# Latent attention: one key product for two heads, and swapped rotary columns among the query weights

## What is computed

```python
def apply_rope(x, cos, sin):
    x1, x2 = jnp.split(x, 2, axis=-1)
    return jnp.concatenate([x1 * c - x2 * s, x2 * c + x1 * s], axis=-1)

def mla_project(q_lat, kv_lat, g_qa, w_qb, g_kva, w_kvb):      # 384 and 256 latents
    q = (rms_norm_2(q_lat, g_qa) @ w_qb).reshape(B, T, 8, 64 + 32)
    kv = (rms_norm_2(kv_lat, g_kva) @ w_kvb).reshape(B, T, 8, 64 + 64)
    return q[..., :64], q[..., 64:], kv[..., :64], kv[..., 64:]
...
qr_x = apply_rope(qr_x, cos_b, sin_b)                          # 32 rotary columns of a head's query
kr_x = apply_rope(krb_x[:, :, None, :], cos_b, sin_b)[:, :, 0] # 32 rotary columns, one key for all heads
s = einsum(q_n, keys_n) + einsum(q_r, keys_r)                  # 64 + 32 = 96 columns
o = softmax(s * 96 ** -0.5) @ vals
```

## Time and profile before

| what | us |
| --- | --- |
| three runs | 3919.3, 3922.16, 3916.91 |
| their median | 3919.3 |
| the profiled execution, its own time | 3926.21 |
| its span, from the first to the last instruction | 3924.3 |

### The profile page before, as it was taken

How to read it: one execution, slowest core, us unless ns; L and a number is a source line. 1 busy time by engine, 2 the same in 40 slices (tenths; PEclk the granted TensorE clock), 3 DMA queues, 4 the chain that set the end, 5 groups by cost and what they waited for, 6 DMA issues and landing times.

```text
span 3924.3 us, 54000 instructions
## 1 busy us (share of the span) xinstructions
PE 3676.7 (94%) x21015; PEld 3094.3 (79%) x21015; DVE 2169.5 (55%) x4547; ACT 1419.9 (36%) x2285; POOL 761.6 (19%) x645
## 2 busy tenths in 40 slices
PE   6989998979999997999997999999999879999997
PEld 4877886869898997999985568868888645776885
DVE  3353343598998667777874463274343345436443
ACT  3223323324444442333333452263222335425322
POOL 0000000007987864555530000000000000000000
PEclk8999999999999999999998999999999989989998
DMA  5223323458787889999971001101111210210222
GB/s 214 92 76 140 102 97 119 156 188 288 272 306 265 300 306 364 347 343 344 372 286 54 33 28 59 60 1 54 65 65 60 102 33 33 73 62 22 97 98 85
DMA packets 220555, 594.49 MB, mean 151 GB/s; under 512 B 17936, under 2 KB 101520, under 8 KB 215952
## 3 DMA queue, kind: packets, MB, share of 16 engines
q1 hardware_dynamic: 156592, 380.68, 28.3%
q0 software_dynamic: 36864, 134.23, 9.5%
q10 hardware_dynamic: 26848, 76.14, 5.1%
HBM read 530.16 MB, written 60.82 MB: 151 GB/s over the span
## 4 chain that ended last, share of the span: by engine, by line
PE 79%; DVE 9%; DMA 7%; issue 2%; ACT 2%; POOL 1%; ACTq 0%; DVEq 0%; SPq 0%
PE bank L735 62%; PE bank L934 6%; DMA WR<-in_vrows 4%; PE bank L1028 3%; PE bank L1014 3%; PE bank L901 2%; DVE WL L1502 1%; PE bank L759 1%; PE bank L796 1%; DMA rows<-in_urows,rk 1%; POOL rows L666 1%; DMA WR<-in_weights 1%; DMA rows<-in_vrows,rk 1%; DVE Rw L1763 1%; ACT WH L1119 0%
## 5 line engine op out<-in xcount | busy, mean ns | idle before, releaser
L1502 DVE TENSOR_TENSOR WL<-WR,WH 128x1024 fp32r<-128x1024 f32 x512 | 631.1, 1234 | 821.2 <-ACT WH L1119 767.2
L1119 ACT ACTIVATE WH<-WR 128x1024 fp32r<-128x1024 f32 x512 | 537.0, 1057 | 798.7 <-DMA WR<-in_weights 201.4
L735 PE MATMUL bank<-H2h,WH 128*128 128x512 f32 (+2 forms) x1624 | 578.6, 356 | 4.5 <-DVE H2l L1530 4.5
L735 PE MATMUL bank<-H2h,WL 128*128 128x512 f32 (+2 forms) x1624 | 573.6, 353 | 0.0
L735 PE MATMUL bank<-H2l,WH 128*128 128x512 f32 (+2 forms) x1624 | 573.0, 353 | 0.0
L735 PE MATMUL bank<-Hh,WH 128*128 128x384 f32 (+1 forms) x1440 | 527.5, 366 | 23.6 <-DVE WL L1502 23.5
L735 PE MATMUL bank<-Hh,WL 128*128 128x384 f32 (+1 forms) x1440 | 512.4, 356 | 0.0
L735 PE MATMUL bank<-Hl,WH 128*128 128x384 f32 (+1 forms) x1440 | 511.7, 355 | 0.0
L934 PE MATMUL bank<-ah,WH 128*128 128x384 f32 x1024 | 345.1, 337 | 35.3 <-issue 18.6
L666 POOL DMA_INDIRECT rows<-in_urows,rk x128 | 169.5, 1324 | 968.4 <-DVE rk L1788 744.4
L735 PEld LDWEIGHTS bank<-H2h,WH 128*128 128x128 f32 (+1 forms) x1624 | 307.0, 189 | 52.5 <-issue 7.7
(11 more groups left out here) (310 smaller groups left out, 5778.8 us busy)
## 6 DMA issues: line engine op xcount, KB each, us to landing
WR<-in_weights SPq DMA_DIRECT2D x498, 512.0 KB, 3.8
WR<-in_vrows SPq DMA_DIRECT2D x128, 512.0 KB, 9.2
gelu_by_expert<-geU ACTq DMA_DIRECT2D x128, 192.0 KB, 5.0
gates_by_expert<-tab ACTq DMA_DIRECT2D x24, 1024.0 KB, 6.4
geV<-gelu_by_expert SPq DMA_DIRECT2D x32, 768.0 KB, 11.8
Gt<-gates_by_expert SPq DMA_DIRECT2D x16, 1536.0 KB, 18.5
x_kept<-X ACTq DMA_DIRECT2D x2, 3072.0 KB, 8.7
X<-x_kept ACTq DMA_DIRECT2D x2, 3072.0 KB, 11.3
```

The costliest lines, as they stand in the source:

```text
L735: yield nc.tensor.matmul(b[0:rows, out_cols], a, r, start=n == 0, stop=n == len(pairs) - 1)
L1119: act.activation(WH[:, n % SLOTS, :, :].rearrange("p a b -> p (a b)"), WR[:, c % SLOTS, :, :].rearrange("p a b -> p (a b)"), ACT.Copy)\
L1502: v.tensor_tensor(WL[:, n % SLOTS, :, :].rearrange("p a b -> p (a b)"), WR[:, plan.splits[n] % SLOTS, :, :].rearrange("p a b -> p (a b)"), ...
```

## The change

The query weights of a head get 32 more columns: the rotary columns again, with their halves swapped. The query product of x so has 128 rows, and rows 96 to 127 are what the permutation product gave, apart from a sign, which goes into the sin table. DVE reads both parts from the bank. The same is done for the shared rotary key. The jobs `hqp` and `krbp`, the matrix `permB`, its load, and the copies to `R4` are gone, and the banks of `hq` and `krb` for x belong to DVE now. The key product is made for two heads at a time, at even h, with 128 rows; ACT copies the upper half into the slot of head h + 1 and the lower half into that of head h. A second tile of two key slots, `KH2`, is added, so that four heads' keys have room. A chunk is still loaded for every head.

```diff
@@ CONSTS
-CONSTS = [("ident", 128), ("perm128", 128), ("permA", 128), ("permB", 96), ("iota128", 128), ("fold", 3)]
+CONSTS = [("ident", 128), ("perm128", 128), ("permA", 128), ("iota128", 128), ("fold", 3)]
@@ make_plan, project
             p.chunk(("hb", l, h), ("hb", l, h), False)
-            p.job(("hq", l, h, "x"), "A")
+            p.job(("hq", l, h, "x"), "V", [] if upd or h % 2 == 0 else [("hb", l, h)])
             if upd:
-                p.job(("hq", l, h, "c"), "A")
-            p.job(("hk", l, h, "x"), "A")
-            p.job(("hk", l, h, "c"), "A", [("hb", l, h)])
-            p.job(("hqp", l, h), "V")
+                p.job(("hq", l, h, "c"), "A", [] if h % 2 == 0 else [("hb", l, h)])
+            if h % 2 == 0:
+                p.job(("hk", l, h, "x"), "A")
+                p.job(("hk", l, h, "c"), "A", [("hb", l, h)])
@@ make_plan, queries_b
-            p.job(("krb", l, "x"), "A")
+            p.job(("krb", l, "x"), "V")
             p.job(("krb", l, "c"), "A", [("krb", l)])
-            p.job(("krbp", l), "V")
@@ build
+        KH2 = place("KH2", B0 + 19200, 2, A)
...
+        def keys_of(h):
+
+            return (KH, KH2)[h % 4 // 2][:, h % 2, :]
@@ PE, project
-                    wq = w[:, 0:QL * QKB].rearrange("p (k n) -> p k n", k=QL)
-                    wk = w[:, QL * QKB:QL * QKB + KVL * NOPE].rearrange("p (k n) -> p k n", k=KVL)
+                    wq = w[:, 0:QL * P].rearrange("p (k n) -> p k n", k=QL)
+                    wk = w[:, QL * P:(QL + KVL) * P].rearrange("p (k n) -> p k n", k=KVL)
                     for c in xc:
+                        rows_ = P if c == "x" else QKB
                         product(("hq", l, h, c), slice(0, T if c == "x" else C),
-                                [(wq[:, j, :], LAT[:, j, xcols(c)]) for j in range(QL)], QKB)
-                    for c in ("x", "c"):
+                                [(wq[:, j, 0:rows_], LAT[:, j, xcols(c)]) for j in range(QL)], rows_)
+                    for c in ("x", "c") if h % 2 == 0 else ():
                         product(("hk", l, h, c), slice(0, T if c == "x" else C),
-                                [(wk[:, j, :], LAT[:, QL + j, xcols(c)]) for j in range(KVL)], NOPE)
-                    pe.wait_ge(act_read, k.reading(act_read, ("hq", l, h, "x")))
-                    product(("hqp", l, h), slice(0, T),
-                            [(consts["permB"][0:QKB, 0:QKB], R4[0:QKB, h % 3, :])], QKB)
+                                [(wk[:, j, :], LAT[:, QL + j, xcols(c)]) for j in range(KVL)])
@@ PE, latents
-                    linear(("krb", l, c), ("krb", l), H2, xcols(c), QKB)
-                pe.wait_ge(act_read, k.reading(act_read, ("krb", l, "x")))
-                product(("krbp", l), slice(0, T), [(consts["permB"][0:QKB, 0:QKB], R4[0:QKB, 0, :])], QKB)
+                    linear(("krb", l, c), ("krb", l), H2, xcols(c), P if c == "x" else QKB)
@@ ACT, project
-                    if h >= 3:
-                        act.wait_ge(dve_read, dve_at(("hqp", l, h - 3)))
                     elif h == 0:
-                        act.wait_ge(dve_read, dve_at(("krbp", l)))
-                    out_of(("hq", l, h, "x"), R4[0:QKB, h % 3, :], slice(0, T), rows=QKB)
+                        act.wait_ge(kx_ready, k.next(kx_ready))
                     if upd:
                         out_of(("hq", l, h, "c"), QH[0:QKB, h % 2, T:A], slice(0, C), rows=QKB)
-                    for c in ("x", "c"):
-                        out_of(("hk", l, h, c), KH[0:NOPE, h % 2, xcols(c)], slice(0, T if c == "x" else C), rows=NOPE)
-                    act.activation(KH[NOPE:QKB, h % 2, :], KR[NOPE:QKB, 0, :], ACT.Copy).then_inc(kr_ready, k.inc(kr_ready))
+                    for c in ("x", "c") if h % 2 == 0 else ():
+                        n_ = T if c == "x" else C
+                        act.wait_ge(filled, filled_at(("hk", l, h, c)))
+                        act.activation(keys_of(h + 1)[0:NOPE, xcols(c)],
+                                       bank[plan.by_key[("hk", l, h, c)].bank][NOPE:2 * NOPE, 0:n_], ACT.Copy)\
+                            .then_inc(act_step, k.inc(act_step))
+                        act.wait_ge(*k.own())
+                        out_of(("hk", l, h, c), keys_of(h)[0:NOPE, xcols(c)], slice(0, n_), rows=NOPE)
+                    act.activation(keys_of(h)[NOPE:QKB, :], KR[NOPE:QKB, 0, :], ACT.Copy).then_inc(kr_ready, k.inc(kr_ready))
@@ ACT, latents
-                out_of(("krb", l, "x"), R4[0:QKB, 0, :], slice(0, T), rows=QKB)
@@ DVE, project
-                    dve.wait_ge(act_read, act_at(("hq", l, h, "x")))
+                    b = bank_of(("hq", l, h, "x"))
...
-                    v.tensor_tensor(QH[0:QKB, h % 2, 0:T], R4[0:QKB, h % 3, :], cosB[0:QKB, :], ALU.mult)\
+                    v.tensor_tensor(QH[0:QKB, h % 2, 0:T], b[0:QKB, :], cosB[0:QKB, :], ALU.mult)\
                         .then_inc(dve_step, k.inc(dve_step))
-                    v.tensor_tensor(t_[0:QKB, 0:T], bank_of(("hqp", l, h))[0:QKB, :], sinB[0:QKB, :], ALU.mult)\
+                    v.tensor_tensor(t_[NOPE:QKB, 0:T], b[QKB:P, :], sinB[QKB:P, :], ALU.mult)\
                         .then_inc(dve_read, k.inc(dve_read))
                     dve.wait_ge(*k.own())
                     dve.wait_ge(kr_ready, k.next(kr_ready))
-                    v.tensor_tensor(QH[0:QKB, h % 2, 0:T], QH[0:QKB, h % 2, 0:T], t_[0:QKB, 0:T], ALU.add)\
+                    q_ = QH[NOPE:QKB, h % 2, 0:T]
+                    v.tensor_tensor(q_, q_, t_[NOPE:QKB, 0:T], ALU.add)\
                         .then_inc(qk_ready, k.inc(qk_ready))
@@ lay_chunk
+        out[:, :, QKB:P] = np.roll(out[:, :, NOPE:QKB], ROPE // 2, axis=2)
...
-        out[:, 0:QL * QKB] = tiles_of(a["w_qb_2"][l][:, h * QKB:(h + 1) * QKB])
-        w = a["w_kvb_2"][l][:, h * (NOPE + VB):h * (NOPE + VB) + NOPE]
-        out[:, QL * QKB:QL * QKB + KVL * NOPE] = tiles_of(w)
+        w = a["w_qb_2"][l][:, h * QKB:(h + 1) * QKB]
+        out[:, 0:QL * P] = tiles_of(np.concatenate([w, np.roll(w[:, NOPE:], ROPE // 2, axis=1)], axis=1))
+        if h % 2 == 0:
+            w = np.concatenate([a["w_kvb_2"][l][:, g * (NOPE + VB):g * (NOPE + VB) + NOPE] for g in (h, h + 1)], axis=1)
+            out[:, QL * P:(QL + KVL) * P] = tiles_of(w)
```

More of the change, by code:

```diff
@@ L493, in build @@
         inv_ready = sem("inv_ready")
-        qk_ready = sem("qk_ready")
+        qk_ready, kx_ready = sem("qk_ready"), sem("kx_ready")
         kr_ready = sem("kr_ready")
@@ L999, in attend @@
                                     pe.wait_ge(qk_ready, k.next(qk_ready))
-                                q, kk = col(QH[0:QKB, h % 2, :], qb), KH[0:QKB, h % 2, :]
+                                q, kk = col(QH[0:QKB, h % 2, :], qb), keys_of(h)[0:QKB, :]
                             if hi > lo:
@@ L2065, in branch @@
                     merge(b)
-                dve.wait_ge(act_read, act_at(("krb", l, "c")))
-                v.tensor_tensor(KR[0:QKB, 0, 0:T], R4[0:QKB, 0, :], cosB[0:QKB, :], ALU.mult)\
+                b = bank_of(("krb", l, "x"))
+                v.tensor_tensor(KR[NOPE:QKB, 0, 0:T], b[NOPE:QKB, :], cosB[NOPE:QKB, :], ALU.mult)\
                     .then_inc(dve_step, k.inc(dve_step))
-                b = bank_of(("krbp", l))
-                v.tensor_tensor(QH[0:QKB, 0, 0:T], b[0:QKB, :], sinB[0:QKB, :], ALU.mult)\
-                    .then_inc(dve_step, k.inc(dve_step))
+                v.tensor_tensor(QH[NOPE:QKB, 0, 0:T], b[QKB:P, :], sinB[QKB:P, :], ALU.mult)\
+                    .then_inc(dve_read, k.inc(dve_read))
                 dve.wait_ge(*k.own())
-                v.tensor_tensor(KR[0:QKB, 0, 0:T], KR[0:QKB, 0, 0:T], QH[0:QKB, 0, 0:T], ALU.add)\
-                    .then_inc(dve_read, k.inc(dve_read))
+                v.tensor_tensor(KR[NOPE:QKB, 0, 0:T], KR[NOPE:QKB, 0, 0:T], QH[NOPE:QKB, 0, 0:T], ALU.add)\
+                    .then_inc(kx_ready, k.inc(kx_ready))
                 for c in xc:
@@ L2224, in shape_constants @@
     f = np.float32
-    consts = np.concatenate([np.eye(P, dtype=f), swap(P, 64), swap(P, 32), swap(QKB, 16, NOPE),
+    consts = np.concatenate([np.eye(P, dtype=f), swap(P, 64), swap(P, 32),
                              np.tile(np.arange(P, dtype=f), (P, 1)),
@@ L2250, in shape_constants @@
     tab2 = np.concatenate([np.tile(ca, (4, 1)), np.tile(sa, (4, 1)), np.concatenate([one, cb, cb, pad]),
-                           np.concatenate([zero, sb_, sb_, pad]), band], axis=1)
+                           np.concatenate([zero, pad, -sb_, sb_]), band], axis=1)
     return consts, tab1, tab2
```

## The result

The changed kernel takes 3884.7 us (median of 5 runs, 3879.2 to 3897.9) against 3922.2 us (3916.9 to 3948.5) of the kernel before on the same chip: ratio 0.991, 95% interval 0.9882 to 0.9939. Forecast were 3883.5 us and -35.8 us; the medians differ by 37.5 us.

What follows compares the result with a forecast made beforehand. PE was taken to bound the kernel: 36.6 us removed from its queue, 1.3 given back and 0.5 saved at the start make -35.8 us, from a median of 3919.3 to 3883.5 us, range 3877 to 3892.

Steps and rivals of the forecast that it cites:

- The price of a pass: In the latent attention stages, one PE pass was priced at 0.460 us over 512 columns and 0.217 us over 256.
- The permutation: Removing each head's permutation product from PE was to save 0.93 us, 8 a layer: 7.4 us a layer.
- Widened on PE: nothing: Query products over 128 instead of 96 weight columns and key products over 128 instead of 64 were to cost PE nothing.
- Given back: 1.3 us: At the latent stages' starts, PE was to wait 0.5 us in layer 0, about 0.2 and 0.55 us in layer 1.
- The start: 0.5 us, bound 1: One constant transfer less at kernel start was to save 0.5 us, between 0 and 1.
- ACT and DVE in the even projection: In layer 0's even projections, the longer copy chain was to leave PE a 0.6 us margin, costing nothing in steady state.
- the even heads stall: Rival, chance 0.12: longer waits between ACT's copies lose 0.5 to 1 us in even projections; -30 us, 3889.
- weight loads show: Rival, chance 0.05: longer weight loads add to every widened PE pass, 8.2 us together, giving 3891.7 us.
- More than forecast: Rival, chance 0.08: the shared key's permutation counts after all and the constants bring 1 us; -38.3, 3881 us.
- The clock falls: Rival, chance 0.12: new PE idle time before the squares or at stage starts halves the clock; 3886 to 3890 us.
- the prediction is wrong if the periods shrink and the total doesn't: Stated test: shorter head periods in the latent stages without a shorter total refute it, since later stages are PE-bound too.

Runs made afterwards that it cites:

- the wide keys: The kernel before with every head's key product made over 128 weight columns instead of 64, upper half unused: 3935.0 us, 1.0006 to the kernel before.
- the earlier copy: The changed kernel with ACT copying the shared rotary key first in a projection and PE waiting for ACT's key copies itself: 3900.3 us, 0.9921 to the kernel before.

## Why the prediction was right, and what of it was off

The mechanism and the sum held: PE bounds the heads, and what leaves its queue leaves the time. The stages were forecast to give 36.6 - 1.3 = 35.3 us and gave 37.2. Its terms, against the text on record:

- **The price of a pass** was too high: 0.427 to 0.430 us from one start to the next over 512 columns and 0.214 over 256, not 0.460 and 0.217. The 20 passes of 6.77 us are 6.41 by these prices, and 0.36 belonged to the group as such, 0.24 of it to its products over 64 weight columns (6.53 us with 128); the division laid it all on the long passes. After, 8 key passes are the difference of two groups, (6.55 - 3.98) = 2.57 us in layer 0, and an even head outlasts an odd one by 2.58 in both layers (20.69 - 18.11, 16.96 - 14.38), where the forecast had 2.71.
- **The permutation** is worth 0.81 us, not 0.93: part of its 0.93 us belonged to the products over 64 weight columns ahead of it, behind wide ones it took 0.86.
- **Widened on PE: nothing** is where a term was missing. It should be -0.31 us a head, 5.0 us in all. A head after an even projection lost 1.15 us (0.81 + 0.31 = 1.12 by the experiments), after an odd one 3.73 (1.12 + 2.58 = 3.70). A stage then is 8 x 1.12 + 4 x 2.58 = 19.3 us, less 0.63 and 0.80 us of waits: 18.7 and 18.5, measured 18.8 and 18.4. The two terms too high come to 1.0 and 1.9 us over both layers, the missing one to 5.0. That they leave only some 2 us is luck.
- **Given back: 1.3 us** measured 1.43.
- **The start: 0.5 us, bound 1** is not shown. PE goes on 0.1 us sooner (16.18 us for 16.27), since the last constant landed no sooner after its issue (11.9 us against 11.58). By 200 us the profiled execution is ahead by 1.1 us, but the second profile of the changed kernel is where the kernel before is (196.78 and 196.77 us at the same product). Over all profiles the kernels with the matrix are there at 196.1 to 197.5 us, those without at 194.9 to 197.4: some 0.6 us apart on average, within a spread of more than 1 us.
- **ACT and DVE in the even projection.** ACT's and DVE's timelines after, for the head whose projection starts at 2224.57:

```profile
2230.45 0.59 ACT L1378 ACTIVATE KH<-bank 64x512 f32<-64x512 f32 x1 [1.28 <-PE bank L739]
2231.08 0.59 ACT L1145 ACTIVATE KH<-bank 64x512 f32<-64x512 f32 x1
2231.70 0.38 ACT L1378 ACTIVATE KH<-bank 64x256 f32<-64x256 f32 x1
2232.11 0.38 ACT L1145 ACTIVATE KH<-bank 64x256 f32<-64x256 f32 x1
2232.51 0.84 ACT L1383 ACTIVATE KH<-KR 32x768 f32<-32x768 f32 x1
...
2235.49 0.93 ACT L1415 ACTIVATE SrowB<-SrowB,nm 128x768 f32<-128x768 f32 x1 [1.74 <-DVE nm L2001]
```

```profile
2233.45 0.68 DVE L1963 TENSOR_TENSOR QH<-QH,rk 32x512 f32<-32x512 f32 x1 [4.59 <-ACT KH L1383]
```

By their ends from that start: copy of the shared key +8.78 (forecast +8.95), add +8.88 by its start (+9.0), exponential from +10.92 (+10.9) to +11.85; PE takes it at +12.43 (+12.65). With the forecast's 0.2 us for the handover to PE the margin is 0.4 us for 0.6. The wait between two copies of a pair is 0.03 to 0.04 us for 0.08, so *the even heads stall* is refuted.

Of the other rivals, *weight loads show* is refuted and reversed. A load takes 190 ns and stays under the shortest pass, 214 ns. The rule of the Trainium skill, "TensorE: Matmul & The Clock Gate", section "LDWEIGHTS (loading the stationary operand)", holds here in what it says of the load, which grows with the weight columns (163 ns at 96 columns, 190 at 128). That the load also sets the spacing stands in another section of that title of the Trainium skill, "Back-to-back issue gap"; it can't be seen in the spacing here, where heads with wider loads are shorter (21.53 us for 21.84). *More than forecast* named 38.3 us for reasons that the runs don't bear out: the shared key's permutation brought nothing, and the start isn't shown to have brought 1 us. *The clock falls* named two places, ahead of the squares and at the starts of the stages, and at neither did it fall; in the stages it stays at 1.00. What took 21.7 us in the profiled execution was the stretch of the earlier trace rows itself, seen before the change, costed only as 4 to 12 us at new places, and never asked how long it can last where it is already. That the median of five fell in the range in spite of it is the luck named with the result. The test "the prediction is wrong if the periods shrink and the total doesn't" would have misled on that execution: -28.3 us, with the sum intact and the clock to blame.

Open stays whether the change makes such a stretch longer or likelier. Runs with a granted clock of 0.960 or less over the span were 11 of 59 of the kernel before and 4 of 11 of the changed one, too few to say. But the other kernels that keep the wait had more of them than the kernel before beside them: the swapped columns alone 7 of 10 and the wide keys 6 of 10, against 5 of 25; the earlier copy 5 of 7, against 2 of 12 (the pair keys alone 3 of 10). So how often the long stretch comes seems to depend on the kernel, by edits that don't touch branch A; no run shows how. Open is also what ends a stretch.

## What to carry to other kernels

Price an edit to a PE-bound stage by differences of starts in a steady head, and get the price of a pass from two neighbouring passes of one shape, not from sums that mix shapes: a division hides the cost of the odd shape in another. Two edits in one chain are worth more or less together than alone: here the pair keys laid a wait bare at the very product that the swapped columns remove. Read the granted clock stage by stage before believing that a busy PE does more work; a wait of 1.5 us that looks too small to mend stood ahead of 22 us lost in branch A of both layers in the profile before, and of 42 us in the profile after.

## What the runs showed of the hardware that was not expected

- PE was granted 1.2 GHz, half its clock, for up to 106 us while it was busy all the time (110.00 of 110.00 us at 0.52), with f32 products of branch A. The clock was truly low, not only recorded so: the 12 passes that take 3.28 us at full clock took 5.39 us where it fell about 1 us into them, 6.02 us where it fell sooner and 6.34 us in the profile of the wide keys (layer 1), whose first 10 us were at 0.50. The Trainium skill, "TensorE: Matmul & The Clock Gate", section "Seeing it yourself", tells of a gate seen stuck at a quarter of the clock for over 50 us and warns not to trust its trace events fully; here it stayed as long at half the clock, and the times bear the events out.
- Filling 1.47 us of idle time with eight products that compute nothing took about 30 us off the time, though they last 2.0 us themselves: 3889.4 to 3859.1 us by medians (ratios 0.991 and 0.9831 to the kernel before, each on its own chip).
- Products over 64 weight columns among ones over 96 made a head 0.31 us longer than the same products over 128, of which half is thrown away (21.84 and 21.53 us in layer 0).
